# One more tile pair as block products in each ConvFFN, with its input sums moved to the first four tiles

## The reference, cut to what matters

```python
def _conv_ffn(x, buf, w_up, conv_w, conv_b, w_down):
    u, v = jnp.split(x @ w_up, 2, axis=-1)          # 1024 -> 2 x 2816
    uc, new_buf = _causal_dwconv(u, buf, conv_w, conv_b)   # width 3
    h = jax.nn.gelu(uc.astype(jnp.float32)) * v.astype(jnp.float32)
    return h.astype(x.dtype) @ w_down, new_buf.astype(buf.dtype)
```

## Time and profile before

| | us |
|---|---|
| median of 3 runs (lowest, highest) | 1376.28 (1376.21, 1377.96) |
| the profiled execution's own time | 1377.05 |
| its span, first to last instruction | 1375.2 |
| TensorE busy | 1355.9 |
| VectorE busy | 956.5 |
| ScalarE busy | 719.5 |
| GpSimd busy | 137.7 |
| granted TensorE clock, mean | 0.997 |

### The profile page before, as it was taken

The page is one execution under the profiler, slowest core; times in us unless marked ns, Lnnn a source line. Parts: engine busy times, 40 slices in busy tenths (PEclk is TensorE's granted clock), DMA queues, the critical chain, the costliest instruction groups (busy, mean ns, idle before and its releaser), DMA issues.

```text
span 1375.2 us, 24844 instructions
## 1 busy us (share of the span) xinstructions
PE 1355.9 (99%) x9868; PEld 1328.5 (97%) x9868; DVE 956.5 (70%) x1499; ACT 719.5 (52%) x1129; POOL 137.7 (10%) x146
## 2 busy tenths in 40 slices
PE   9999999999999999999999999999999999999996
PEld 8999999999999999999999999999999999999996
DVE  6656565655778558844886778888784688448865
ACT  5443544453565347722764568755653467236734
POOL 0020111100230000000000320022300000000002
PEclk9999999999999999999999999999999999999998
DMA  8175597859722235533554259852498955235522
GB/s 327 49 253 178 127 206 196 233 116 289 206 62 73 90 123 162 169 102 98 161 162 139 77 190 205 233 134 98 151 216 236 245 162 174 91 115 162 169 62 85
DMA packets 80899, 217.47 MB, mean 158 GB/s; under 512 B 6928, under 2 KB 9232, under 8 KB 80528
## 3 DMA queue, kind: packets, MB, share of 16 engines
q1 hardware_dynamic: 52560, 138.82, 31.0%
q0 software_dynamic: 27648, 76.03, 22.9%
q10 hardware_dynamic: 576, 1.05, 0.2%
HBM read 208.23 MB, written 74.74 MB: 206 GB/s over the span
## 4 chain that ended last, share of the span: by engine, by line
PE 85%; DVE 7%; ACT 3%; DMA 3%; issue 1%; SPq 1%; DVEq 0%; ACTq 0%
PE PS L768 26%; PE PS L769 25%; PE PS L770 25%; DMA raw<-weights 2%; PE PS L937 1%; PE PS L946 1%; DVE Y L1882 1%; PE PS L952 1%; DVE Y L1870 1%; PE PS L917 1%; PE PS L896 1%; DMA Y<-xP 1%; DVE S L2211 1%; PE PS L926 1%; PE PS L1086 0%
## 5 line engine op out<-in xcount | busy, mean ns | idle before, releaser
L768 PE MATMUL PS<-xhi,whi 128*128 128x296 f32 (+1 forms) x1536 | 469.0, 305 | 1.3 <-DVE wlo L1595 1.2
L769 PE MATMUL PS<-xlo,whi 128*128 128x296 f32 (+1 forms) x1536 | 457.7, 298 | 0.0
L770 PE MATMUL PS<-xhi,wlo 128*128 128x296 f32 (+1 forms) x1536 | 457.4, 298 | 0.0
L1120 ACT ACTIVATE whi<-raw 128x1024 fp32r<-128x1024 f32 (+2 forms) x256 | 253.9, 994 | 202.1 <-PE PS L770 193.5
L1589 DVE TENSOR_TENSOR wlo<-raw,whi 128x1024 fp32r<-128x1024 f32 (+2 forms) x256 | 294.1, 1152 | 65.9 <-ACT whi L1120 56.6
L768 PEld LDWEIGHTS PS<-xhi,whi 128*128 128x128 f32 x1536 | 289.9, 189 | 5.2 <-DVE xlo L2121 1.7
L769 PEld LDWEIGHTS PS<-xlo,whi 128*128 128x128 f32 x1536 | 290.4, 189 | 1.3
L770 PEld LDWEIGHTS PS<-xhi,wlo 128*128 128x128 f32 x1536 | 289.4, 188 | 0.0
L768 PE MATMUL PS<-hhi,whi 128*128 128x296 f32 (+2 forms) x864 | 258.2, 299 | 0.4 <-DVE Y L1807 0.4
L769 PE MATMUL PS<-hlo,whi 128*128 128x296 f32 (+2 forms) x864 | 257.0, 297 | 0.0
L770 PE MATMUL PS<-hhi,wlo 128*128 128x296 f32 (+2 forms) x864 | 256.4, 297 | 0.0
(11 more groups left out here) (270 smaller groups left out, 1679.5 us busy)
## 6 DMA issues: line engine op xcount, KB each, us to landing
raw<-weights SPq DMA_DIRECT2D x118, 512.0 KB, 4.3
weight_sums<-weights POOLq DMA_DIRECT2D x24, 2048.0 KB, 16.9
raw<-weights SPq DMA_DIRECT2D x96, 256.0 KB, 3.4
weight_sums<-weight_sums POOLq DMA_DIRECT2D x8, 2048.0 KB, 10.7
raw<-weight_sums SPq DMA_DIRECT2D x64, 256.0 KB, 3.5
raw<-weight_sums SPq DMA_DIRECT2D x32, 512.0 KB, 4.0
raw<-weights SPq DMA_DIRECT2D x16, 384.0 KB, 3.4
Y<-xP SPq DMA_DIRECT2D x8, 296.0 KB, 7.4
```

The costliest lines, as they stand in the source:

```text
L768: pe.matmul(dst, wh, h, start=first, stop=False, skip_group_check=onto)
L769: pe.matmul(dst, wh, lo, start=False, stop=False, skip_group_check=onto)
L770: return pe.matmul(dst, wl, h, start=False, stop=last, skip_group_check=onto)
L1120: act.activation(high(u, i)[:, 0:n], raw_of(u, i), ACT.Copy).then_inc(w_hi, 1)
```

## The change

`SINGLE` goes from 6 to 4: tiles 4 and 5, the last two of the first group, become a pair. With it:

- the weight sums get a third group in each layer, of two pairs of units (steps of 0.5 MB) besides two groups of eight (2 MB). Layer 0's last group moves from the head phase to GpSimd's work behind layer norm 0; layer 1's first two groups go together behind layer norm 1, its last behind layer norm 2;
- the input sums of row block k are made in tile k, 0 to 3. GpSimd makes the two differences t1, t3, right behind its last low row of x; VectorE only the two rests t2, t4. Two pairs of scratch rows are used in turn (`SUM_ROWS`), so that row blocks 0 and 1 need no wait, and row block k > 1 waits for the low parts of k - 2;
- the low parts of the input sums move behind the gate products of "v"; they now come in the same tile as the sums;
- the low parts of h of tiles 2 and 3 move into the first pair's block, behind its products.

```diff
-SINGLE = 6
+SINGLE = 4
...
+GROUP_OF = [layer * len(GROUPS) + FFN[u - base][2] for layer, base in enumerate((U_FFN0, U_FFN1))
+            for u in PAIRS if base <= u < base + N_FFN]
...
+        SUM_ROWS = ((KEPT, MORE), (6, 7))
...
+            def input_differences(layer, k):
+                w, at = wid(U_FFN1 if layer else U_FFN0), off(U_FFN1 if layer else U_FFN0)
+                pool.wait_ge(ln_x, (4 * layer + 2) * KT)
+                if k > 1:
+                    pool.wait_ge(xt_lo, KT * layer + 2 * k - 2)
+                x11, x12, x22 = Y[:, k, span(0, at)], Y[:, k, span(1, at)], Y[:, KT // 2 + k, span(1, at)]
+                t1, t3 = (columns_of(row, w)[:, 0, :] for row in SUM_ROWS[k % 2])
+                pool.tensor_tensor(t1, x11, x12, ALU.subtract).then_inc(xt_diff, 1)
+                pool.tensor_tensor(t3, x22, x12, ALU.subtract).then_inc(xt_diff, 1)
...
-                if ln:
-                    for step in range(len(SUM_STEPS)):
-                        sum_step(1 + ln, step)
+                if ln != 1:
+                    for k in range(KT // 2):
+                        input_differences(ln // 2, k)
+                for step in range(len(SUM_STEPS)):
+                    for group in ((2,), (3, 4), (5,))[ln]:
+                        sum_step(group, step)
...  ScalarE, "v"
-                        if 1 <= j <= KT // 2:
-                            input_sums_hi(j - 1)
+                        input_sums_hi(j)
...  VectorE, input_sums
-                    done(tt(t1, x[0][0], x[0][1], ALU.subtract))
+                    dve.wait_ge(xt_diff, KT * layer + 2 * k + 2)
                     done(stt(t2, t1, -1.0, x[1][1], ALU.mult, ALU.subtract), xt_sum)
-                    done(tt(t3, x[1][1], x[0][1], ALU.subtract))
                     done(stt(t4, t2, -1.0, x[1][0], ALU.mult, ALU.subtract), xt_sum)
...  VectorE, block_of_pairs
-                    if j > first:
+                    if j > max(first, SINGLE):
...
                     weights_lo(u + 2, 0)
+                    if j == SINGLE:
+                        low_of_h(j - 2, first)
                     pair_rows(n, j, 3)
                     weights_lo(u + 2, 1)
+                    if j == SINGLE:
+                        low_of_h(j - 1, first)
...  VectorE, "v"
-                        if 1 <= j <= KT // 2:
-                            input_sums_lo(j - 1)
...  (the three gate products)
-                        dve.wait_ge(h_hi, hb + j + 1)
-                        done(tt(hlo[:, j - first, at:], s(4 + j % 2, at), hhi[:, j - first, at:].bitcast(F32), ALU.subtract),
-                             h_lo)
+                        input_sums_lo(j)
+                        if j < 2:
+                            low_of_h(j, first)
```

More of the change, by code:

```diff
@@ L188 @@
 PER_LAYER = len(PAIRS) // 2
-PER_GROUP = PER_LAYER // (len(GROUPS) - 1)
+GROUP_OF = [layer * len(GROUPS) + FFN[u - base][2] for layer, base in enumerate((U_FFN0, U_FFN1))
+            for u in PAIRS if base <= u < base + N_FFN]
 RAWS = 4
@@ L433, in trunk @@
         pads = sem("pads_ready")
-        w_sums = [sem(f"weight_sums_of_group{i}") for i in range(2 * (len(GROUPS) - 1))]
+        w_sums = [sem(f"weight_sums_of_group{i}") for i in range(2 * len(GROUPS))]
         h_made = sem("h_of_pair_made")
@@ L438, in trunk @@
         xt_sum, xt_hi, xt_lo = sem("input_sums_made"), sem("input_sums_hi"), sem("input_sums_lo")
+        xt_diff = sem("input_differences_made")
         tapped = sem("first_tap_done")
@@ L612, in load_weights @@
                 n = PAIRS.index(u - second(u))
-                sp.wait_ge(w_sums[n // PER_GROUP], 16 * len(SUM_STEPS))
+                sp.wait_ge(w_sums[GROUP_OF[n]], 16 * len(SUM_STEPS))
                 if second(u):
@@ L675, in sum_step @@
                 first, last = slice(0, HALF), slice(HALF, 2 * HALF)
-                n = group * PER_GROUP
-                units = weights[PAIRS[n]:PAIRS[n] + 2 * PER_GROUP].rearrange("(n t) p c -> t p n c", t=2)
-                sums = W_SUMS[n:n + PER_GROUP].rearrange("n p c -> p n c")
+                n, count = GROUP_OF.index(group), GROUP_OF.count(group)
+                units = weights[PAIRS[n]:PAIRS[n] + 2 * count].rearrange("(n t) p c -> t p n c", t=2)
+                sums = W_SUMS[n:n + count].rearrange("n p c -> p n c")
                 to, source, add = SUM_STEPS[step]
@@ L1391, in input_sums_hi @@
                         act.wait_ge(xt_sum, KT * layer + 2 * k + r + 1)
-                        act.activation(XT[:, 2 * r:2 * r + 2, 0, k, 0:w], columns_of((KEPT, MORE)[r], w),
+                        act.activation(XT[:, 2 * r:2 * r + 2, 0, k, 0:w], columns_of(SUM_ROWS[k % 2][r], w),
                                        ACT.Copy).then_inc(xt_hi, 1)
@@ L1941, in input_sums @@
                     x = [[Y[:, KT // 2 * low_rows + k, span(t, at)] for t in range(2)] for low_rows in range(2)]
-                    (t1, t2), (t3, t4) = ([columns_of(row, w)[:, c, :] for c in range(2)] for row in (KEPT, MORE))
-                    done(tt(t1, x[0][0], x[0][1], ALU.subtract))
+                    (t1, t2), (t3, t4) = ([columns_of(row, w)[:, c, :] for c in range(2)] for row in SUM_ROWS[k % 2])
+                    dve.wait_ge(xt_diff, KT * layer + 2 * k + 2)
                     done(stt(t2, t1, -1.0, x[1][1], ALU.mult, ALU.subtract), xt_sum)
-                    done(tt(t3, x[1][1], x[0][1], ALU.subtract))
                     done(stt(t4, t2, -1.0, x[1][0], ALU.mult, ALU.subtract), xt_sum)
@@ L1953, in input_sums_lo @@
                         dve.wait_ge(xt_hi, KT * layer + 2 * k + r + 1)
-                        done(tt(XT[:, 2 * r:2 * r + 2, 1, k, 0:w], columns_of((KEPT, MORE)[r], w),
+                        done(tt(XT[:, 2 * r:2 * r + 2, 1, k, 0:w], columns_of(SUM_ROWS[k % 2][r], w),
                                 XT[:, 2 * r:2 * r + 2, 0, k, 0:w].bitcast(F32), ALU.subtract), xt_lo)
@@ L2095, in ffn @@
                             lambda_rows()
-                    if kind == "u" and 1 <= j <= KT // 2:
-                        input_sums(j - 1)
+                    if kind == "u":
+                        input_sums(j)
             def lambda_rows():
```

## The result

| | before | after |
|---|---|---|
| median, us (lowest, highest; 13 executions each) | 1376.68 (1375.67, 1378.42) | 1380.81 (1378.72, 1386.17) |
| ratio, 95% interval | | 1.0034 (1.0027 to 1.0042) |
| profiled execution, its own time | 1377.05 | 1380.81 |
| its span | 1375.2 | 1379.0 |
| TensorE matmuls | 9868 | 9820 |

The change makes the kernel slower by 0.34%, 4.1 us. The forecast was 1375.5 us, a little faster than before, in a range of 1372.2 to 1378.6: the measured time is outside that range and on the wrong side. The spread between executions also grew, from 2.8 to 7.5 us.

The account below looks back on a forecast made before the run. TensorE, busy 99% of the span, was taken to bound the kernel. Matmuls -6.4, second-product waits +3.2 and ConvFFN starts +2.4 gave -0.8 us: 1375.5 us from a median of 1376.28, range 1372.2 to 1378.6.

Parts of the forecast that it names:

- Matmuls: Both ConvFFNs: two more tiles as a pair save 3.40 us in layer 0, 3.04 in layer 1, together 6.44.
- First place: Second product of the first pair waits for the last input sums' low halves: 1.62 us a layer, 3.2 together.
- Second place: Start of each ConvFFN: GpSimd's differences and the rests delay VectorE, so TensorE is late at u2 and v2: 2.4 us.
- rival 2: Each GpSimd operation that steps in costs VectorE its whole 0.8 us: 1377.9 us, chance 0.10.
- The DMAs ... at nothing: Moved weight sums beside the ConvFFNs and in the recurrent layer finish in time, queues have room: 0 us.
- rival of relief: Rival 3, head phase: smaller group step removes TensorE's 0.96 us stop before 353.21; -1.9 in all, 1374.4 us, chance 0.10.
- rival 4: Beside the ConvFFNs, weights arrive late under the moved sums: three steps, 2 us each, 1381.5 us; 0.09 with unforeseen waits.
- the point of decision: Tile pairs in the ConvFFNs: late weights decide from a load landing of about 14 us.
- rival 1: Start of the ConvFFNs: GpSimd doesn't hold up VectorE's taps, only the second-product waits stay: 1373.1 us, chance 0.25.

Follow-up runs that it names:

- e10: e8, with the first step of the last group's weight sums issued before row block 2's differences: 1370.31 us, ratio 0.9952 against the kernel before.
- e9: Kernel before, SINGLE still 6, with layer 0's second group of weight sums moved from the head phase to behind layer norm 0: 1376.10 us, ratio 0.9998.
- e8: e7 with e3's edit as well: 1370.87 us, ratio 0.9954 against the kernel before.
- e7: e1, with the eighth step of the last group's sums in both layers held until the last product of tile 13: 1374.54 us, ratio 0.9984 against before.
- e1: Changed kernel, with the head phase's last 2 MB weight-sum step issued only after layer norm 0's low rows and differences: 1379.04 us, ratio 1.0012 against before.
- e2: Kernel before, with the eighth step of its second group issued behind layer norm 0's low rows: 1377.32 us, ratio 1.0000.
- e3: Changed kernel, with the low halves of row block 3's input sums put back in front of tile 3's gate products: 1378.84 us.
- e4: Changed kernel, with all eight pairs of differences on VectorE, none on GpSimd: 1380.40 us, ratio 1.0025 against before.
- e6: Changed kernel, with 24 useless matmuls in front of TensorE's stop in the head phase: 1379.89 us.

## Why the prediction was wrong

**Matmuls, -6.4 us: right.** 48 fewer in the ConvFFNs and none elsewhere. e10 is the changed kernel without most of its side effects: 5.8 us under e9, the kernel before with its own moved group. In their traces the two ConvFFNs with their layer norms take 5.7 us less, with 0.4 us of waits at v2 still in them: some 6.1 of the 6.4.

**First place, +3.2 us: right.** 1.31 and 1.66 us of idle, in full intervals 1.61 and 1.96, 3.3 with the usual 0.14 taken off. e8 got 3.7 back by a change of order: VectorE's idle time lies before the gate products, and the rests may run there.

**Second place, +2.4 us: the mechanism right, the size wrong.** The operations step in at 0.45 us each (0.5 forecast), but TensorE was late by 0.24 and 0.17 us, some 0.5 with the restarts, and not at u2. This term was too high by 1.9 us; the miss of the total is on the other side. Of tile 0's stretch I had 1.65 and it was 1.36, of tile 1's 1.05 and it was 0.83; against 0.45 and 0.24 us of slack such tenths decide. The Trainium skill's rule (SBUF — State Buffer, section "Who interferes with whom") of a lock for the whole instruction fits the direction; rival 2, its full 0.8 us each, does not fit the rows.

**"The DMAs ... at nothing": this step failed, in both its parts.** The forecast priced the moved weight sums at 0 us; after against e7, which differ only in when two kinds of eighth steps are issued, is 6.3 us. In the head phase I saw that the group's step was a quarter as large and that the other "follows it at once", and named it only as a rival of relief with a chance of 0.10. The two halves of that sentence decide the case. What the load meets is 2.5 MB in place of 2, since the second issue, 19.55 us late before, is no longer held. The relief has the wrong sign, and the stop's growth has a second price, the clock. Across the runs: 0.5 MB ahead of the load (e1, e7, e8, e10), no stop; 2 MB, none, 0.32 and 0.96 us (e2, e9, before); 2.5 MB, 3.21, 3.16 and 2.89 us (after, e3, e4).
Beside the ConvFFN I asked only whether the sums would be ready in time, and they were: the first step was issued at 422 ("about 415"), the eighth at 527, landing at about 547 ("by about 530"), long before tile 14; in the recurrent layer the eighth was issued by 902 ("920 at most"). What I priced wrongly is what they meet there: the eighth step falls beside the pairs of tiles 6 to 13, which move 158 GB/s to the 72 of single units. That is rival 4, given 0.09 with unforeseen waits. In e1 median landings of 8.8 and 10.9 us already went with stops, under the 14 us that I set as the point of decision; ahead of e3's stop of 3.09 us they reached 14.4. Most stops are under 2 us each, but there are several. I wrote against it that the kernel before has such traffic with no gap. That traffic ran beside single units and d units but for the last step, which was issued just before the first pair.
In sum, from the medians: after less e1, 1.8 us, e1 less e7, 4.5 us, together 6.3. Without them the change is e7, 1374.5 us. How the 6.3 us divide between the head phase and the pairs differs between executions and is not settled: in after's profiled execution the head phase took 4.9 us and the stops in the pairs 0.4, in e1's the stops in the pairs took 3.2 and the clock 1.7. In e1 layer 0's chain of steps begins behind the moved 2 MB step and so reaches further into the pairs (eighth issue at 538.18, not 527.12), which may be part of it (argued, not tested).

**The range** held the terms at VectorE and none for the DMAs: rival 4's 1381.5 us, 0.7 from what was measured, lay outside it. Its lower end, rival 1 with the relief, adds up to 1372.0 and not 1372.2; nothing hangs on that.

## What to carry to other kernels

A transfer that is made smaller or moved changes what is issued behind it: list the queue's next issue and the load that it meets, and ask in which stage the loads are densest, not only whether the moved work is done in time. Try background transfers beside the stage that loads least; here one wait on a count of products did that, and the median came down by 4.5 us. In a stage that TensorE fills, look also at the order of an in-order engine's work around its idle time: putting two operations ahead of it was worth 3.7 us here (e8 against e7), beside some 6 us for the matmuls taken away.

Read the granted clock over the whole span, and not only at the stop in question: one execution of e1 lost 1.7 us to it in a stage that no edit touched.

## What the runs showed of the hardware

- A stop of TensorE of 3.2 us cost 2.6 us more than itself: the granted clock was 0.50 from 355 to 360 and 0.84 from 360 to 365. In e3 a stop of 3.09 us before 1126.99 had 0.66 in the mean from 1125 to 1130. Stops of 0.96, 1.31, 1.58 and 1.66 us left it at 1.00. But the length of a stop does not tell by itself: behind 1.89 us in e1 the clock was 0.72 from 895 to 900, and behind 2.00 us (before) and 2.40 us (e7) at the same place in the program it was 1.00. In e1 that fall cost 1.7 us. The Trainium skill (TensorE: Matmul & The Clock Gate, section "What's actually happening") says that the clock is throttled by default and that activity releases it; e6, with useless matmuls in the stop, agrees: 1.00 from 350 to 365.
- A load of 0.5 MB issued by SP took 17.23 us to land behind GpSimd's accumulating transfers of 2.5 MB, 15.71 behind 2 MB, and 7.4 behind 0.5 MB (e1). The Trainium skill (DMA: Bandwidth & Descriptors, section "Queues, rings and completion order") says that a DMA engine takes the queues that have work for it in turn; that fits a load held up by another queue's traffic, and the landings here give its size.
- GpSimd could not issue its second accumulating step of 2 MB for 19.55 us before: it came at 349.87, and the first, issued at 328.70, took 20.9 us to land. It issued accumulating steps of 0.5 and 2 MB together in 2.82 us after, and before two steps of 2 MB that only copy in 1.79 us (305.97). So the size and the kind of a transfer also set when the issuing engine is free again.
